# Mixture-of-experts stage of a decoder layer: expert items of 128 rows, with tails of up to 32 rows in plain fp32 on four column groups

## The chip, the cores and the metric

The kernel runs on one core of one Trainium2 chip. The metric is device time in microseconds of one launch of the whole layer. The kernel before takes 2739.65 us, the median of 3 runs (2737.45 to 2740.82). Below, PE is the matrix engine (PEld its weight loads), DVE the vector engine, ACT the scalar engine, POOL the GpSimd engine and SP the sync engine, which here issues the weight DMAs.

## The reference

One decoder layer on 1024 tokens of 1024 channels, in fp32: dilated attention beside a causal convolution, an output projection, a mixture of 32 experts of which each token takes 4, and a per-layer embedding at the end. Only the mixture of experts changes:

```python
logits = (xt @ w_router + b_router).astype(jnp.float32)
top_val, top_idx = lax.top_k(logits, TOP_K)          # 4 of 32 experts a token
gates = jax.nn.softmax(top_val, axis=-1)
...                                                   # tokens are grouped by expert
gu = rows @ w_gate_up[e] + b_gate_up[e]               # (rows, 1024) @ (1024, 2048)
gate = jnp.minimum(gu[:, :D_FF], SWIGLU_LIMIT)
up = jnp.clip(gu[:, D_FF:], -SWIGLU_LIMIT, SWIGLU_LIMIT)
hid = (up + 1.0) * (gate * jax.nn.sigmoid(gate * SWIGLU_ALPHA))
return hid @ w_down[e] + b_down[e]                    # (rows, 1024) @ (1024, 1024)
```

Each row of an expert's result goes back to its token, times its gate. 1024 tokens times 4 give 4096 rows over 32 experts, 128 a piece in the mean. With the reference's own inputs the counts of the experts 0 to 31 are 133, 123, 110, 68, 179, 71, 131, 118, 88, 121, 203, 58, 81, 65, 249, 125, 94, 133, 109, 240, 126, 118, 149, 112, 160, 135, 167, 130, 23, 235, 109, 133 (worked out from the reference on the host; they give 46 blocks of 128, as many as the trace shows row stores).

## The kernel before, in words

The stages run one after the other: input norm and projections, attention with the convolution beside it, output projection and router (until about 780 us), experts (780 to 2526 us), output (to the end). Names and lines below are those of the listing at the end of this section.

**Items.** After the router, DVE builds a table of items from the counts (lines 1817 to 1862): an item is an expert with up to 256 of its rows (`BLK`), that is one or two blocks of 128. Every engine walks the same table in a loop (`Items.run`, line 473): two outer steps of `GROUP` = 32 items each, the second skipped when item 32 is not alive, and an inner `If` for each item that isn't. `TWO` says that an item has a second block, and for it the engine runs the body with blocks `(1, 0)`, otherwise with `(0,)`. Here there are 32 items, 14 of them with two blocks.

**Pieces.** The weights of an item come in 12 pieces of 1 MB into 6 buffers `raw`: pieces 0 to 7 are half of the contraction for 256 gate and 256 up columns (`gate_piece`), pieces 8 to 11 a quarter of the contraction of the down projection (`down_piece`). SP loads a piece when DVE has read its buffer (line 978). A matmul of fp32 precision is made of three in a faster format: ACT rounds a piece to `whi` (`split_hi`, line 1447, up to 6 ahead), DVE takes the difference to `wlo` (`split_lo`, line 709, up to 4 ahead), the rows are split in the same way (`xhi`, `xlo`), and `three` (lines 550 to 552) multiplies hi by hi, lo by hi and hi by lo. A block therefore takes, for each item, 12 matmuls of 128x512 a piece, a bias row (line 544) for each of six results, 8 transposes of its rows (`turn_rows`, line 521) and 8 of its hidden values (`turn_hidden`, line 529).

**Order.** It is written out by hand as steps c = 0 to 11 on every engine. After piece c, PE gives `w_free`; on that ACT splits piece c + 6 and DVE piece c + 4. Between these splits stand, in the same order for each item, the clamps, the sigmoid (ACT), the gating (DVE) and the split of the turned hidden values. ACT and DVE are in-order, so a split that waits holds up the small operations behind it. POOL fetches the row numbers and gathers the rows of the next item (lines 1069 and 1071), and ACT stores the results of a block (`rows_out`, line 1476).

Of the kernel before, what the change touches and what calls it, by code (L numbers as in the profile page):

```python
# [18 lines left out]
P = 128  # L19
# [27 lines left out]
BLK = 2 * P  # L47
MAX_ITEMS = E + T * TOPK // (BLK + 1)
# [27 lines left out]
def layer(nc, x, p_in, positions, g_mix_pre, w_in, w_dw, b_dw, g_conv_ln, b_conv_ln, w_out, g_mix_post,  # L76
# [3 lines left out]
    with outer:  # L80
# [10 lines left out]
        def banks(b, n=1):  # L91
# [5 lines left out]
        list_dram = nc.dram_tensor("token_list", (E * T, 1), I32, kind="Internal").ap()  # L97
        y_dram = nc.dram_tensor("expert_rows", (MAX_BLOCKS * P, D), F32, kind="Internal").ap()
# [112 lines left out]
        xhi = sb("xhi", [P, 2, KD, P], F32R)  # L211
        xlo = sb("xlo", [P, 2, KD, P], F32R)
        hhi = sb("hhi", [P, 2, KD, P], F32R)
        hlo = sb("hlo", [P, 2, KD, P], F32R)
        xg = sb("xg", [P, 2, D])
        ysb = sb("ysb", [P, 2, D])
        gat = sb("gat", [P, 2, 256])
        upc = sb("upc", [P, 2, 256])
        sig = sb("sig", [P, 2, 256])
        hid = sb("hid", [P, 2, 2, 256])  # L220
        bsp = sb("bsp", [P, 3 * D], F32R)
        one_r = sb("one_r", [P, P], F32R)
        ids = sb("ids", [P, 2], I32)
# [108 lines left out]
        gu_done = sem("gu_done1")  # L332
        gu_used = [sem(f"gu_used{b}") for b in range(2)]
        gat_ready = [sem(f"gat_ready{b}") for b in range(2)]
        sig_done = [sem(f"sig_done{b}") for b in range(2)]
        gs_done = [sem(f"gs_done{b}") for b in range(2)]
        hid_ready = [sem(f"hid_ready{b}") for b in range(2)]
        ht_done = [sem(f"ht_done{b}") for b in range(2)]
        hhi_ready = [sem(f"hhi_ready{b}") for b in range(2)]
        hlo_ready = [sem(f"hlo_ready{b}") for b in range(2)]  # L340
        y_done = [sem(f"y_done{b}") for b in range(2)]
        y_used = [[sem(f"y_used{b}{d}") for d in range(2)] for b in range(2)]
        y_out = [sem(f"y_out{b}") for b in range(2)]
        ids_in = [sem(f"ids_in{b}") for b in range(2)]
        xg_in = [sem(f"xg_in{b}") for b in range(2)]
        xt4_done = [sem(f"xt4_done{b}") for b in range(2)]
        xhi_ready = [sem(f"xhi_ready{b}") for b in range(2)]
        xlo_ready = [sem(f"xlo_ready{b}") for b in range(2)]
# [30 lines left out]
        ITEM_MAX = {EXPERT: E - 1, ROW: E * T - BLK, TWO: 1, NTWO: MAX_ITEMS, LIVE: 1, BEFORE: MAX_ITEMS,  # L379
                    YROW: (MAX_BLOCKS - 2) * P}  # L380
# [12 lines left out]
        TWO_STEP = 37  # L393
        TABLE_STEP = 43
# [64 lines left out]
        class Items:  # L459
# [17 lines left out]
            def run(self, body):  # L477

                eng = self.eng
                with eng.Fori(0, 2) as o:  # L480
                    with eng.If(read(eng, o * GROUP, LIVE) > 0):
                        with eng.Fori(o * GROUP, o * GROUP + GROUP) as n:
                            live, two = self.value(LIVE), self.value(TWO)
                            k1 = eng.snap(self.twos, min_val=0, max_val=MAX_ITEMS)
                            with eng.If(live > 0):
                                with eng.If(two > 0):
                                    body(n, k1, (1, 0))
                                    eng.reg_add(self.twos, self.twos, 1)
                                with eng.Else():
                                    body(n, k1, (0,))  # L490

        def gate_bank(blocks, b, q):
            return banks(2 * b + q % 2) if len(blocks) == 2 else banks(2 + q % 2)

        def down_bank(b, d):
            return banks(2 * b + d)
# [13 lines left out]
        def experts_pe(pe):  # L510

            pe.wait_ge(bias_zero, 2)

            def turn_rows(b, k, other, before):

                pe.wait_ge(xg_in[b], 16 * k + 16)

                if before is not None:
                    pe.wait_ge(xlo_ready[other], before)
                for j in range(KD):  # L520
                    mm = pe.transpose(banks(4, 2)[:, j * P:j * P + P], xg[:, b, j * P:j * P + P], ident)  # L521
                mm.then_inc(xt4_done[b], 1)
# [1415 lines left out]
```

## Time and profile before

| | |
|---|---|
| median of 3 runs | 2739.65 us (2737.45 to 2740.82) |
| profiled execution, its own time | 2739.35 us |
| its span (first to last instruction) | 2737.7 us |
| busy PE / DVE / ACT / POOL | 2504.0 / 1736.6 / 1316.9 / 200.8 us |
| granted TensorE clock, mean of the span | 0.961 of 2.4 GHz (1.00 in the expert stage from 840 us) |
| chain that ended last, share by engine | PE 80%, DVE 7%, issue 6%, DMA 3% |
| moved by DMA | 556.34 MB, mean 203 GB/s |

How to read it: an engine's busy time is what its own instructions take, without waits; matmuls overlap, so a matmul that is listed with 390 ns may start 227 ns after the one ahead of it. The chain is followed back from the last instruction, at each step to what released it; its shares say where a shorter instruction would have shortened the whole. The share of the DMA engines is a mean over 16; where it stands at 1.00 or above, transfers wait for each other.

### The profile page before, as it was taken

The numbers are of one execution on the slowest core, as the hardware profiler recorded it, in microseconds if no ns is written. First come the engines' busy times: TensorE is split into PE (matmuls) and PEld (weight loads), VectorE is DVE, ScalarE is ACT, GpSimd is POOL, SyncE is SP. The second block draws the span as 40 slices with busy tenths as digits, with TensorE's granted clock in tenths as the row PEclk, the third lists the DMA queues.
The fourth block names the chain that finished last, engine by engine and source line by source line (L and its number), as shares of the span: only waits on it lengthen the run. The fifth ranks groups of instructions, "written<-read, shape, count | busy, mean of one in ns | idle before, by whom it ended". The sixth has DMA issues, their size and how long they took to land.

```text
span 2737.7 us, 36956 instructions
## 1 busy us (share of the span) xinstructions
PE 2504.0 (91%) x10955; PEld 1803.4 (66%) x10956; DVE 1736.6 (63%) x2495; ACT 1316.9 (48%) x1535; POOL 200.8 (7%) x188
## 2 busy tenths in 40 slices
PE   7999999768829999999999999999999999998687
PEld 3454555434428778787877878787878888776343
DVE  4664555623356986779688696778675667674454
ACT  2113344422124775567477574666554445562232
POOL 1100100002220000000000000000000000000210
PEclk9999999888859999999999999999999999999799
DMA  5009610333225996789699696879675667783541
GB/s 178 20 12 334 197 28 13 110 104 69 61 93 170 348 343 218 253 285 369 211 340 343 224 339 214 293 250 334 219 268 201 207 206 241 244 284 132 181 144 50
DMA packets 387537, 556.34 MB, mean 203 GB/s; under 512 B 18241, under 2 KB 326977, under 8 KB 387362
## 3 DMA queue, kind: packets, MB, share of 16 engines
q1 hardware_dynamic: 333922, 456.55, 50.2%
q10 hardware_dynamic: 39408, 57.67, 5.8%
q0 software_dynamic: 14160, 41.51, 4.5%
q8 instruction: 27, 0.44, 0.1%
q14 instruction: 20, 0.16, 0.0%
HBM read 482.91 MB, written 71.19 MB: 202 GB/s over the span
## 4 chain that ended last, share of the span: by engine, by line
PE 80%; DVE 7%; issue 6%; DMA 3%; ACT 2%; SPq 1%; DVEq 1%; ACTq 0%; POOLq 0%; POOL 0%
PE bank L552 16%; PE bank L550 16%; PE bank L551 16%; PE bank L1120 6%; PE bank L1264 5%; PE bank L645 4%; PE bank L1143 3%; PE bank L1110 2%; PE bank L544 2%; PE bank L1160 2%; PE bank L1189 2%; PE bank L1175 1%; PE bank L521 1%; PE bank L529 1%; DVE wlo L709 1%
## 5 line engine op out<-in xcount | busy, mean ns | idle before, releaser
L1447 ACT ACTIVATE whi<-raw 128x2048 fp32r<-128x2048 f32 x384 | 733.1, 1917 | 578.0 <-PE bank L552 531.8
L709 DVE TENSOR_TENSOR wlo<-raw,whi 128x2048 fp32r<-128x2048 f32 x384 | 875.9, 2285 | 209.2 <-PE bank L552 194.1
L550 PE MATMUL bank<-whi,xhi 128*128 128x512 f32 x1472 | 577.1, 392 | 0.0
L552 PE MATMUL bank<-wlo,xhi 128*128 128x512 f32 x1472 | 574.3, 390 | 0.0
L551 PE MATMUL bank<-whi,xlo 128*128 128x512 f32 x1472 | 573.7, 390 | 0.0
L552 PEld LDWEIGHTS bank<-wlo,xhi 128*128 128x128 f32 x1472 | 276.4, 188 | 58.2
L551 PEld LDWEIGHTS bank<-whi,xlo 128*128 128x128 f32 x1472 | 276.6, 188 | 57.0
L550 PEld LDWEIGHTS bank<-whi,xhi 128*128 128x128 f32 x1472 | 276.9, 188 | 54.2
L550 PE MATMUL bank<-whi,hhi 128*128 128x512 f32 x736 | 292.2, 397 | 0.0
L552 PE MATMUL bank<-wlo,hhi 128*128 128x512 f32 x736 | 287.4, 391 | 0.0
L551 PE MATMUL bank<-whi,hlo 128*128 128x512 f32 x736 | 286.9, 390 | 0.0
L725 DVE TENSOR_SCALAR gat<-bank 128x256 f32<-128x256 f32 x184 | 77.7, 422 | 149.2 <-PE bank L552 149.2
L552 PEld LDWEIGHTS bank<-wlo,hhi 128*128 128x128 f32 x736 | 138.1, 188 | 29.7
L551 PEld LDWEIGHTS bank<-whi,hlo 128*128 128x128 f32 x736 | 138.4, 188 | 27.1
L550 PEld LDWEIGHTS bank<-whi,hhi 128*128 128x128 f32 x736 | 138.4, 188 | 25.8
L1264 PE MATMUL bank<-uT,mixS 128*128 128x512 f32 x256 | 129.4, 670 | 16.8 <-DMA gffn<-in_g_ffn_pre_dram 16.8
L645 PE MATMUL bank<-raw,h2T 128*128 128x512 f32 x256 | 120.1, 625 | 19.4 <-DVE ple L829 16.6
L1069 POOL DMA_DIRECT2D ids<-token_list x46 | 26.1, 568 | 1345.2 <-PE bank L521 1314.2
L544 PE MATMUL bank<-bsp,one_r 128*128 128x512 f32 x276 | 116.1, 421 | 0.4 <-issue 0.4
L1645 DVE CUSTOM_DVE_ANT_0 S<-bank,mlog 128x512 f32<-128x512 f32 (+3 forms) x144 | 72.9, 553 | 64.1 <-PE bank L1160 41.0
L1264 PEld LDWEIGHTS bank<-uT,mixS 128*128 128x128 f32 x256 | 54.9, 218 | 86.1 <-issue 86.1
L1364 ACT ACTIVATE PT<-bank 128x512 f32<-128x512 f32 (+3 forms) x96 | 44.5, 514 | 136.5 <-PE bank L1175 136.5
(261 smaller groups left out, 2837.9 us busy)
## 6 DMA issues: line engine op xcount, KB each, us to landing
raw<-in_w_gate_up_dram SPq DMA_DIRECT2D x512, 512.0 KB, 4.5
raw<-in_w_down_dram SPq DMA_DIRECT2D x128, 1024.0 KB, 5.8
expert_rows<-zeros ACTq DMA_DIRECT2D x1, 32768.0 KB, 103.5
expert_rows<-ysb ACTq DMA_DIRECT2D x46, 512.0 KB, 6.2
xall<-in_x_dram SPq DMA_DIRECT2D x8, 512.0 KB, 10.5
uT<-in_w_out_dram SPq DMA_DIRECT2D x1, 4096.0 KB, 13.3
xr<-in_x_dram SPq DMA_DIRECT2D x8, 512.0 KB, 6.8
h_scratch<-h SPq DMA_DIRECT2D x8, 512.0 KB, 2.7
```

Of the source, the lines that this page charges most:

```text
L544: mm = pe.matmul(dst, one_r[:], bsp[:, q * 512:q * 512 + 512], start=True, stop=False)
L550: pe.matmul(dst, stat_hi[:, b, kt], hi, start=False, stop=False)
L551: pe.matmul(dst, stat_lo[:, b, kt], hi, start=False, stop=False)
L552: return pe.matmul(dst, stat_hi[:, b, kt], lo, start=False, stop=last)
L645: pe.matmul(banks(4 + half), h2T[:, k], wpg[:, k, half * 512:half * 512 + 512], start=(k == 0), stop=(k == KD - 1))
L709: dve.tensor_tensor(wlo[:, c % LO], raw[:, c % RAW], whi[:, c % HI].bitcast(F32), ALU.subtract).then_inc(lo_ready, 1)
L725: dve.tensor_scalar(gat[:, b], src[:, 0:256], LIMIT, None, ALU.min).then_inc(gat_ready[b], 1)
L1120: mm = pe.matmul(banks(bank_no), w[:, k], uT[:, k, half * 512:half * 512 + 512], start=(k == 0), stop=(k == KD - 1))
L1143: mm = pe.matmul(banks(b + c)[:, 0:n], uT[:, k, t * P:t * P + P], wv[:, k, c * 512:c * 512 + n], start=(k == 0), stop=(k == KD - 1))
L1264: mm = pe.matmul(banks(2 * s + half), mixS[s][:, k], wout[:, k, half * 512:half * 512 + 512], start=(k == 0), stop=(k == KD - 1))
L1447: act.activation(whi[:, c % HI], raw[:, c % RAW], ACT.Copy).then_inc(hi_ready, 1)
L1645: dve.tensor_tensor_reduce(out=S[b][:, c * 512:c * 512 + w], in0=banks(2 * c + h)[:, 0:w], in1=mlog[:, T - n + c * 512:T - n + c * 512 + w ...
```

## The change: what it does

An item is now one block of up to 128 rows, and may have a tail of up to 32 rows. An expert with n rows gets ceil(n / 128) items, but where its last one would hold 32 rows or fewer they go as a tail with the item ahead of it (the thresholds are 160, 288, ... instead of 256, 512, ...). `TWO` and `NTWO` now say whether there is a tail and how many came before. The second set of row buffers is gone, and with it the body for two blocks.

The tail takes the weights straight from `raw` in plain fp32, without the split. It has 32 rows, so its transposed rows are a weight load of 128x32, and four such products stand beside each other on the four groups of 32 columns of the array: in pieces 0 to 7 group j takes contraction tile j of the piece, all four give partial sums of the same 512 columns, and a further matmul with a constant `sel` adds the four; in pieces 8 to 11 group j takes output columns 256j to 256j + 255. Gate and down biases come by DMA into `bias_t` and `bias_d`. The tail's piece c + 4 (`AHEAD`) follows main piece c on PE; tail pieces 0 to 3 therefore stand in pieces 8 to 11 of the item ahead, under an `If`. SP frees a buffer when the tail has read it, too. The list of token numbers, the results' buffer and a few table steps grow accordingly.

```diff
-BLK = 2 * P
-MAX_ITEMS = E + T * TOPK // (BLK + 1)
+TAIL = 32
+GROUPS = P // TAIL
+MAX_ITEMS = E + T * TOPK // (P + TAIL + 1)
...
+        XT, SUM, HT, ACC = 4, 5, 6, 7
+        AHEAD = 4
...
+            def tail_piece(n, k1, c):
+                pe.wait_ge(hi_ready, PIECES * n + c + 1)
+                if c == 0:
+                    pe.wait_ge(xt_ready, k1 + 1)
+                    pe.wait_ge(ytail_ready, k1)
+                if c in (2, 4, 6, 8):
+                    pe.wait_ge(sums_ready, 4 * k1 + c // 2)
+                if c >= 8:
+                    pe.wait_ge(ht_ready, 4 * k1 + c - 7)
+                if c < 8:
+                    half = c % 2
+                    for j in range(GROUPS):
+                        mm = pe.matmul(banks(ACC)[j * TAIL:j * TAIL + TAIL, :], xt[:, half * 4 + j], raw[:, c % RAW, j],
+                                       start=(half == 0), stop=(half == 1))
+                else:
+                    r = c - 8
+                    for kk in range(2):
+                        for j in range(GROUPS):
+                            mm = pe.matmul(banks(ACC)[j * TAIL:j * TAIL + TAIL, 0:256], htail[:, 2 * r + kk],
+                                           raw[:, c % RAW, 2 * kk + j // 2, j % 2 * 256:j % 2 * 256 + 256],
+                                           start=(r == 0 and kk == 0), stop=(r == 3 and kk == 1))
+                mm.then_inc(tail_free, 1)
+            def tail_sum(n, k1, j):
+                pe.wait_ge(sums_ready, 4 * k1 + j + 1)
+                pe.wait_ge(xlo_ready, n + 1)
+                pe.wait_ge(hid_t_ready, 4 * k1 + j)
+                pe.matmul(banks(SUM)[0:TAIL, :], sel[:], sums[:], start=True, stop=True).then_inc(u_done, 1)
+            def turn_tail_hidden(k1, j):
+                hold(pe, hid_t_ready, 4 * k1 + j + 1)
+                hold(pe, ht_ready, 4 * k1 + j)
+                for h in range(2):
+                    mm = pe.transpose(banks(XT)[:, h * TAIL:h * TAIL + TAIL], hid_t[0:TAIL, h * P:h * P + P],
+                                      ident[0:TAIL, 0:TAIL])
+                mm.then_inc(htt_done, 1)
...
+            def body(n, k1, tail):                                  # PE
+                nk1 = k1 + tail
+                for c in range(PIECES):
+                    pe.wait_ge(lo_ready, PIECES * n + c + 1)
+                    mm = gate_piece(n, c) if c < 8 else down_piece(n, c)
+                    mm.then_inc(w_free, 1)
+                    if c in (3, 5, 7):
+                        turn_hidden(n, (c - 3) // 2)
+                    if tail and c in (0, 2, 4, 6):
+                        turn_tail_hidden(k1, c // 2)
+                    if tail and c in (0, 2, 4):
+                        tail_sum(n, k1, c // 2 + 1)
+                    if tail and c + AHEAD < PIECES:
+                        tail_piece(n, k1, c + AHEAD)
...
+                    if c + AHEAD >= PIECES:
+                        with pe.If(nxt2 > 0):
+                            tail_ahead(n + 1, nk1, c + AHEAD - PIECES)
...
+            def tail_sums(k1, j):                                   # DVE
+                if j == 0:
+                    dve.wait_ge(bias_t_in, 16 * k1 + 16)
+                dve.wait_ge(u_done, 4 * k1 + j)
+                dve.wait_ge(tail_free, PIECES * k1 + 2 * j + 2)
+                dve.tensor_tensor(sums[:].rearrange("p (h n) -> p h n", h=2),
+                                  banks(ACC).rearrange("p (h n) -> p h n", h=2),
+                                  bias_t[:].rearrange("p (h q n) -> p h q n", h=2, q=4)[:, :, j, :],
+                                  ALU.add).then_inc(sums_ready, 1)
...
+                    if tail and c in (1, 3, 5):
+                        tail_gated(k1, (c + 1) // 2)
+                    if tail and c in (1, 3):
+                        tail_sums(k1, (c + 3) // 2)
+                    if tail and c in (0, 2, 4):
+                        tail_clamp(k1, c // 2 + 1)
...
+                                read_by_tail = sp.snap(tails * PIECES + two * (c + 1), ...)   # SP
+                                hold(sp, lo_ready, PIECES * n + c + 1)
+                                sp.wait_ge(tail_free, read_by_tail)
...
+            pool.memset(bias_t[:], 0.0).then_inc(tail_zero, 1)      # POOL, once
```

ACT has a copy for each turned tail tile (`tail_columns`, `tail_hidden`), a sigmoid for each quarter (`tail_sigmoid`) and four DMAs for a tail's result. `tail_clamp`, `tail_gated` and `tail_rows` on DVE are the counterparts of `clamp`, `gated` and the copy of the result.

On PE, in the body for an item with a second part, this stands behind the first piece (lines 550 to 552 are `three`, 544 the bias row). Before, the same piece is run for block 0:

```order
L552 MATMUL bank<-wlo,xhi 128x512
L560 REGISTER_ALU [waits y_used00]
L544 MATMUL bank<-bsp,one_r 128x512 [waits bias_in0,xlo_ready0]
L550 MATMUL bank<-whi,xhi 128x512
L551 MATMUL bank<-whi,xlo 128x512
L552 MATMUL bank<-wlo,xhi 128x512
```

After, in its place (583 is the last line of `three`, 652 turns the tail's hidden values, 646 adds its partial sums, 630 is its piece 4, x3 after the one that waits):

```order
L583 MATMUL bank<-wlo,xhi 128x512
L420 ISA
L652 MATMUL bank<-cst,hid_t 128x32 [waits hid_t_ready,ht_ready]
L652 MATMUL bank<-cst,hid_t 128x32
L643 REGISTER_ALU
L646 MATMUL bank<-sums,sel 32x512 [waits hid_t_ready,xlo_ready,sums_ready]
L619 REGISTER_ALU
L630 MATMUL bank<-raw,xt 32x512 [waits sums_ready,hi_ready]
L630 MATMUL bank<-raw,xt 32x512 x3
```

Thirteen matmuls of 128x512 have gone; seven small instructions, two of which wait for DVE, have come.

On DVE, the same body, step c = 1. Before (709 is the split of the weights, 725 and 726 the clamps, 730 and 737 the gating):

```order
L725 TENSOR_SCALAR gat<-bank 128x256 [waits hid_ready0]
L726 TENSOR_SCALAR upc<-bank 128x256
L708 REGISTER_ALU [waits w_free]
L709 TENSOR_TENSOR wlo<-raw,whi 128x2048 [waits hi_ready]
L730 TENSOR_TENSOR sig<-gat,sig 128x256 [waits sig_done1]
L737 SCALAR_TENSOR_TENSOR hid<-upc,sig 128x256 [waits ht_done1,gs_done1]
```

After (803 and 804 clamp, 790 splits the weights, 841 and 845 gate the tail, 827 takes its partial sums):

```order
L803 TENSOR_SCALAR gat<-bank 128x256 [waits hid_ready]
L804 TENSOR_SCALAR upc<-bank 128x256
L789 REGISTER_ALU [waits w_free]
L790 TENSOR_TENSOR wlo<-raw,whi 128x2048 [waits hi_ready]
L841 TENSOR_TENSOR sig_t<-gat_t,sig_t 32x256 [waits sig_t_done]
L845 SCALAR_TENSOR_TENSOR hid_t<-upc_t,sig_t 32x256 [waits htt_done,gs_t_done]
L826 ISA [waits u_done]
L827 TENSOR_TENSOR sums<-bank,bias_t 128x512 [waits tail_free]
```

The tail's gating and sums now stand behind a split of 2.3 us on the same engine.

## Rows read from the trace of the kernel before

**Rows 1.** Groups by line, 800 to 2526 us: busy, mean ns | idle before, releaser.
```profile
L709 DVE TENSOR_TENSOR wlo<-raw,whi 128x2048 fp32r<-128x2048 f32 x384 | 875.9, 2285 | 209.2 <-PE bank L552 194.1 <-issue 14.3
```
**Rows 2.** ACT timeline: row stores of items 4, 5, 6 to 9, 24, 25; end.
```profile
1079.06 0.34 ACTq L1476 DMA_DIRECT2D expert_rows<-ysb  x1
...
1119.40 0.35 ACTq L1476 DMA_DIRECT2D expert_rows<-ysb  x1
...
1189.74 0.34 ACTq L1476 DMA_DIRECT2D expert_rows<-ysb  x1
...
1226.65 0.42 ACTq L1476 DMA_DIRECT2D expert_rows<-ysb  x1
...
1263.62 0.41 ACTq L1476 DMA_DIRECT2D expert_rows<-ysb  x1
...
1305.86 0.35 ACTq L1476 DMA_DIRECT2D expert_rows<-ysb  x1
...
2083.75 0.34 ACTq L1476 DMA_DIRECT2D expert_rows<-ysb  x1
...
2156.49 0.34 ACTq L1476 DMA_DIRECT2D expert_rows<-ysb  x1
...
2524.46 1.28 ACT L658 ACT_TABLE_LOAD   x1 [3.98 <-issue]
```
**Rows 3.** Windows: us, PE PEld DVE ACT POOL busy, clock, DMA share, GB/s.
```profile
1226.65:1263.62 36.97, 36.65 (x168) 29.48 (x167) 34.91 (x34) 29.89 (x25) 2.52 (x3) 1.00 1.07 370
...
2132.00:2205.00 73.00, 72.30 (x335) 59.55 (x334) 44.72 (x55) 34.69 (x38) 2.53 (x3) 1.00 0.61 201
...
960.00:1020.00 60.00, 56.30 (x257) 45.35 (x256) 49.01 (x46) 42.48 (x36) 4.21 (x5) 1.00 1.02 353
```
**Rows 4.** PE timeline in a block: two matmuls in a row.
```profile
1227.05 0.39 PE L552 MATMUL bank<-wlo,xhi 128*128 128x512 f32 x1
1227.28 0.39 PE L550 MATMUL bank<-whi,xhi 128*128 128x512 f32 x1
```
**Rows 5.** The DMA view, 1226 to 1263 us: rate in 40 slices, packets.
```profile
GB/s 357 331 324 321 380 422 425 412 421 416 412 412 412 412 403 407 421 380 374 350 349 347 350 350 344 349 351 344 350 351 358 334 327 344 352 344 350 352 350 373
DMA packets 9710, 13.65 MB, mean 369 GB/s; under 512 B 416, under 2 KB 8367, under 8 KB 9708
```
**Rows 6.** Timelines of item 9: ACT waits for a load, DVE for ACT.
```profile
1271.05 1.92 ACT L1447 ACTIVATE whi<-raw 128x2048 fp32r<-128x2048 f32 x1 [1.68 <-DMA raw<-in_w_gate_up_dram]
...
1274.73 0.42 DVE L730 TENSOR_TENSOR sig<-gat,sig 128x256 f32<-128x256 f32 x1 [3.14 <-ACT sig L1455]
```
**Rows 7.** PE timeline in attention: plain fp32 matmuls (out columns * rows).
```profile
243.55 1.98 PE L1120 MATMUL bank<-uT,wk 128*128 128x512 f32 x4
245.37 0.27 PE L1175 MATMUL bank<-cst,S 128*128 128x128 f32 x1
...
247.64 1.53 PE L1189 MATMUL bank<-PT,raw 128*64 128x128 f32 x24
249.10 1.12 PE L1120 MATMUL bank<-uT,wk 128*128 128x512 f32 x2
```
**Rows 8.** Groups by form on PE, whole span: plain fp32 matmuls alone.
```profile
L1120 PE MATMUL bank<-uT,wq 128*128 128x512 f32 x192 | 91.7, 605 | 0.1
...
L1143 PE MATMUL bank<-xall,uT 128*128 128x256 f32 x128 | 28.9, 379 | 0.0
```
**Rows 9.** Groups by form on DVE, expert stage: small operations.
```profile
L737 DVE SCALAR_TENSOR_TENSOR hid<-upc,sig 128x256 f32<-128x256 f32 x184 | 78.3, 425 | 6.3
...
L714 DVE TENSOR_TENSOR xlo<-bank,xhi 128x1024 fp32r<-128x1024 f32 x46 | 56.2, 1221 | 19.4 <-ACT xhi L1451 19.4
```
**Rows 10.** PE timeline at the stage's start: the second turn waits for its gather.
```profile
817.40 1.97 PE L521 MATMUL bank<-cst,xg 128*128 128x128 f32 x8 [6.47 <-DMA xg<-u_scratch,ids]
819.74 0.79 PE L544 MATMUL bank<-bsp,one_r 128*128 128x512 f32 x1 [0.37 <-issue]
```
**Rows 11.** PE's waits, 822 to 2520 us.
```profile
PE bank L521 <- DVE xlo L714: 19.8, 13, 1.8
```

More of the change, by code:

```diff
@@ L331, in layer @@
         w_free = sem("w_free")
[L332 to L348, printed above, removed]
+        gu_used = sem("gu_used")
@@ L747, in experts_dve, with body @@
             for c in range(LO):
                 split_lo(0, c)
+            columns(0)
             with dve.If(items.value(TWO) > 0):
-                columns(1, 0)
-            columns(0, 0)
-            def body(n, k1, blocks):
-                nk1 = k1 + (len(blocks) - 1)
+                for c in range(AHEAD):
+                    tail_ahead(0, c)
+            def body(n, k1, tail):
+                nk1 = k1 + tail
                 for c in range(PIECES):
+                    if tail and c == 8:
+                        tail_rows(k1)
@@ L1478, in _, with tail_rows_out @@
+            def tail_rows_out(k1, row):
+                act.wait_ge(ytail_ready, k1 + 1)
+                for j in range(GROUPS):
+                    act.dma_start(y_dram[bass.ds(row + P, TAIL), j * 256:j * 256 + 256],
+                                  ysb_t[j * TAIL:j * TAIL + TAIL]).then_inc(ytail_out, 16)
             items = Items(act, "act", (LIVE, TWO))
             for c in range(HI):
+                if c == 4:
+                    with act.If(items.value(TWO) > 0):
+                        tail_columns(0)
+                    columns(0)
@@ L1517, in body @@
                         nxt, nxt2 = items.value(LIVE), items.value(TWO)
-                    if c == 10:
+                    if tail and c == 9:
+                        tail_rows_out(k1, row)
+                    if c == 11:
                         with act.If(nxt2 > 0):
-                            columns(0, n + 1)
+                            tail_sigmoid(nk1, 0)
             items.run(body)
-            stored = [read(act, P - 1, what) * 16 for what in (BEFORE, NTWO)]
-            for b in range(2):
-                act.wait_ge(y_out[b], stored[b])
+            stored = read(act, P - 1, BEFORE) * 16, read(act, P - 1, NTWO) * 64
+            act.wait_ge(y_out, stored[0])
+            act.wait_ge(ytail_out, stored[1])
             act_fin(act)
```

471 lines of the change are left out of this document (273 added, 198 removed).

## The prediction

> **What bounds the kernel now.** I read the page first: PE 80% of the chain that ended last, so PE it is; then the marks of the items, then windows over single items. The change touches the expert stage alone. Its PE work runs from the first bias row at 819.74 us to the last block's end, about 2519.9 us, just ahead of the end of ACT's last copy (2524.46 - 3.98) [rows 2, 10]: 1700 us. In it stand 32 items, 18 of one block and 14 of two, 46 blocks. What a block costs is read from the stores. Items 24 and 25, both of two blocks, end 2156.49 - 2083.75 = 72.74 us apart, 36.4 a block; item 8, of one block, takes 1263.62 - 1226.65 = 36.97 us [rows 2]. 46 x 36.4 = 1674, and 26 us are left; most are one wait: where a two-block item follows, PE waits for DVE's xlo (19.8 us, 13 times) [rows 11].
>
> So PE is full in both kinds of item (36.65 busy of 36.97, 72.30 of 73.00) [rows 3], with a matmul each 0.227 us [rows 4]. But with one block there is no slack elsewhere either: DVE is busy 34.9 us of 36.97, and the DMA share stands at 1.07, against 0.61 with two blocks [rows 3]. The loads of one item need 13.65 MB in 37 us, at 350 GB/s in the gate pieces and about 412 in the down pieces [rows 5]. A third item of one block in a row shows what comes of it: ACT waits 1.68 us for a load, its sigmoid is late, DVE waits 3.14 us for that [rows 6].
>
> **The change part by part.**
>
> *Items.* By the counts in the reference section 14 experts have over 128 rows. Eight have 160 or fewer (0, 6, 17, 22, 24, 25, 27, 31) and get one item with a tail; six (4, 10, 14, 19, 26, 29) get two items and load their weights twice. So 38 items instead of 32, 38 blocks instead of 46, 8 tails. 30 items have no tail. Per PE the eight blocks save 8 x 36.4 = 291 us, and per DMA six loads more are 82 MB. DMA was at 0.61 with two blocks; now most items are of the kind that needs all of it.
>
> *An item without a tail.* The first after slack takes 36.9 (1226.65 - 1189.74), the second 36.97 [rows 2]. The third (item 9) took 42.24 to its store, but that holds the ending before a two-block item, with its xlo wait; item 5, the same ending with no one-block item ahead, took 1119.40 - 1079.06 = 40.34 [rows 2], so 1.9 us is what the late sigmoid cost. That makes 38.8. From the fourth on, DMA sets the pace: 13.65 MB at the 369 GB/s of this window is 37.0 us, and at the 353 GB/s of a mixed window [rows 3, 5] 38.7; I take 37.4, near the window that is all of one item. The order of experts gives runs without a tail of 6, 12, 5, 1, 2 and 4 items: 225 + 449 + 187.5 + 37 + 74 + 150 = 1122 us. The xlo wait goes with the second set of rows: now the rows are turned at c = 7 and needed at the next item's c = 0. New branches on PE I cost at nothing: the branches behind c = 7 and c = 9 of today leave it busy for 36.65 of 36.97 us [rows 3], so its sequencer reads ahead.
>
> *A tail on PE.* Three rows bound a plain fp32 matmul. Four of 128x512 start at 243.55 and the next thing at 245.37: 0.43 us each with the change-over, so twice 512 columns at 2.4 GHz. 24 of 64 columns of weights and 128 moving, in two column groups, take 249.10 - 247.64 = 1.46 us, 0.061 each, where one in the whole array takes 0.107 by the same two cycles a column: two groups do run side by side [rows 7]. Four groups are not in the trace. Bounds for the four matmuls of a tail piece: 0.43 us, if side by side, and 4 x 0.43 = 1.7, one after the other. I take 0.43, as the two groups behave, and 0.2 for changing in and out of the narrow form (1.46 - 24 x 0.054 = 0.16 in the row named). 12 pieces x 0.63 = 7.6 us (a down piece has eight of 256 columns, two rounds of 0.215, the same). Four sums at 0.43 + 0.1: 2.1. 16 turns of 32 rows at 0.06 and five change-overs: 2.0. Together 11.7 us.
>
> The Trainium skill (FP8 and Floating Point Precision, on true fp32) says that it makes 4 passes through the array; the row above shows the time of two. By the page's figure the 12 pieces and 4 sums would take 16 x 0.43 = 6.9 us more a tail, and the whole 55 us more, about 2647. The Trainium skill (TensorEngine Tiling, key properties) also says that changing the tiling mode drains the engine; that is the change-over above, and the trace agrees that it is small.
>
> *The tail's waits.* Each quarter goes PE pieces, DVE sums, PE sum, DVE clamp, ACT sigmoid, DVE gating, PE turn, ACT copy, and DVE and ACT reach their parts only behind a split of 2.29 and 1.92 us [rows 1, 6]. Counted from the end T of the item ahead: ACT stores and splits, then the tail's sigmoid ends at T + 3.9, DVE's gating (two of 0.42 [rows 9]) at T + 4.75, its sums (0.65, half of the 1.22 for 1024 columns) at T + 5.4. PE is there after tail piece 3 and main piece 0 at T + 3.6: it waits 1.6 us. At c = 2 the same count gives 1.5 (the sigmoid's table load, 1.28 like the one in [rows 2], stands in the way), at c = 4 0.5 and at c = 6 0.3. 3.9 us together, bounds 0 and twice that. DVE has 34.9 + 8.6 us of work in some 52, so it is not the bound of a tail item.
>
> A tail item is therefore 36.9 + 11.7 + 3.9 = 52.5 us, the tail 15.6. Eight: 420 us.
>
> *Start and end.* DVE's table has five steps more and POOL sets bias_t: 3 us ahead of the first fetch. At the start PE waited for the second gather (turned from 817.40) [rows 10]. Now the tail's rows are that second gather, and behind them stand four tail pieces with a trip to DVE, before main piece 0: 7 us more, less the 3 us of tail work that the 420 already hold. Outer step two has 6 live items and 26 dead ones, each three or four instructions of the sequencer, which no row shows; the last store's landing hides the first 3.98 us of that [rows 2]. I take 3 us, bounds 0 and 10. POOL's fetches for a tail, its broadcasts and the four stores move 0.64 MB beside an item of 52 us: nothing. SP's wait on the tail costs nothing, since the tail reads a buffer 4 pieces before the main rows, at the time of DVE's split.
>
> *Sum.* 1122 + 420 - 3 + 7 + 3 + 3 = 1552 us against 1700: 148 us less. The profiled execution's own 2739.35 (span 2737.7 and 1.65 around it) is 0.3 below the median of the runs, so 2739.5 - 148 = 2592 us.
>
> **The rivals.**
>
> *The loads bound every item.* For it: share 1.07, ACT's wait for loads in the second and third item of a run. Against: 369 GB/s is just what an item needs. Runs of 6 and 12 items have no double block to refill the buffers. At 353 GB/s, 38.7 us an item: 30 x 1.3 = 39 more, 2631. Long waits in the tail's round (doubled, 31 us) give the same, 2623.
>
> *The tail is cheaper.* ACT and DVE slip ahead and PE never waits for them, and no item without a tail takes over 37: 31 + 15 less, 2546.
>
> *Column groups take turns.* Weight loads of four groups or the shared bank keep them apart. 32 x 0.43 + 32 x 0.215 = 20.6 instead of 5.2 us a tail: 8 x 15.4 = 123 more, 2715. Against: the two groups of attention.
>
> *Slower than before.* Place: the tail pieces on PE. Mechanism: the groups neither overlap nor pipeline, since all write one bank, so each matmul takes its full 605 or 379 ns [rows 8]: 32 x 0.605 + 32 x 0.379 = 31.5 instead of 5.2, 8 x 26.3 = 210 more, 2802. It decides from 18.5 us more a tail on. For it: four groups accumulate into the same bank. Against: attention's 24 do so in pairs at 0.061 each.
>
> *The change doesn't do what it says:* other counts on the chip, so more items or fewer tails. The 46 blocks and the places of the two-block items agree with the counts, so I give it nothing of its own.
>
> **How the numbers follow.** Forecast 2592 (its own range 2565 to 2620): 52%. Loads or waits longer, 2620 to 2665: 21%. Cheaper tail, 2540 to 2565: 13%. Groups in turn: 7%. The page's four passes, 2647: 2%, against the row. Slower: 5%. The range 2545 to 2660 leaves out the last two large cases and some of the edges. Faster by over 0.2% 94%, within 0.2% (what a measurement of this kernel can tell from no change) 1%, slower 5%.
>
> **What would show it.** 38 row stores in the stage, runs of them 37 to 39 us apart, tail items 50 to 55; DMA share at 1 nearly throughout and clock at 1.00. Tail matmuls of 32x512: four starting within 0.5 us. PE's waits: none for xlo, some 30 us for the tail's gating and sums. I am wrong if one-block items settle well over 38 us, if four tail matmuls take over 1 us, or if PE's waits in a tail item pass 8 us.

## The result, and the profile after

Before: 2740.24 us median of 4 runs (2737.45 to 2741.53). After: 2652.10 us median of 4 (2651.18 to 2655.26). The ratio is 0.9682 with a 95% interval of 0.9665 to 0.9698: 88 us less, where 148 were forecast. The time lies inside the range of 2545 to 2660, near its upper end, and 60 us above the forecast of 2592. The profiled execution took 2655.26 us with a span of 2653.3; its working below is made against its own time, 63.9 us above the forecast's 2591.35 for such an execution.

In the page after, PE is busy for 90% of the span, and the chain of waits still runs mostly over it, with issue (an engine that waits for nothing the profile shows) second:

```profile
PE 2386.5 (90%) x10843; PEld 1603.3 (60%) x10844; DVE 1884.2 (71%) x2573; ACT 1452.9 (55%) x1604; POOL 242.4 (9%) x229
...
PE 69%; issue 10%; DVE 9%; DMA 5%; ACT 4%; DVEq 1%; SPq 1%; ACTq 1%; POOL 0%; POOLq 0%
```

What answers to the row stores of [rows 2] is ACT's timeline again. First the stores around one tail item: the tail's four (x4), then the item's own, then those of two items without a tail.

```profile
1161.13 2.16 ACTq L1636 DMA_DIRECT2D expert_rows<-ysb_t  x4
1167.01 0.36 ACTq L1630 DMA_DIRECT2D expert_rows<-ysb  x1
1203.95 0.37 ACTq L1630 DMA_DIRECT2D expert_rows<-ysb  x1
1241.84 0.35 ACTq L1630 DMA_DIRECT2D expert_rows<-ysb  x1
...
2027.26 0.36 ACTq L1630 DMA_DIRECT2D expert_rows<-ysb  x1
...
2080.09 0.36 ACTq L1630 DMA_DIRECT2D expert_rows<-ysb  x1
```

There are 38 such stores. The first item after a tail takes 36.94 us, the next 37.89; a tail item after another takes 2080.09 - 2027.26 = 52.83; an item ahead of a tail, which holds four of its pieces, takes about 43.0 (an item ended at 2117.03 and the next, ahead of a tail, at 2160.08). The windows, with the columns of [rows 3] (us; PE, PEld, DVE, ACT, POOL busy; clock, DMA share, GB/s), of one item, of a tail item with four pieces of the next tail, and of ten items without one:

```profile
1203.95:1241.84 37.89, 36.88 (x168) 29.42 (x167) 34.87 (x34) 30.01 (x25) 2.59 (x2) 1.00 1.05 364
1970.00:2027.00 57.00, 54.77 (x317) 34.11 (x315) 42.94 (x55) 31.83 (x34) 4.46 (x7) 1.00 0.72 241
1205.00:1575.00 370.00, 361.42 (x1632) 288.77 (x1631) 341.75 (x328) 295.25 (x247) 23.00 (x20) 1.00 1.05 363
```

PE is busy for 361.42 of 370 us without tails, so 0.87 us of an item is idle, where [rows 3] had 0.32 in one. The new groups on PE, by form, 780 to 2450 us:

```profile
L630 PE MATMUL bank<-raw,xt 128*32 128x512 f32 x512 | 86.0, 615 | 0.0
...
L636 PE MATMUL bank<-raw,htail 128*32 128x256 f32 x512 | 39.0, 385 | 0.0
L646 PE MATMUL bank<-sums,sel 128*32 128x512 f32 x64 | 33.5, 605 | 2.1 <-DVE sums L827 0.9
L652 PE MATMUL bank<-cst,hid_t 32*128 32x32 f32 x64 | 9.1, 222 | 15.9 <-DVE hid_t L845 15.9
```

Here the counts are the thing to see. Eight tails have eight gate pieces of four matmuls, which is 256 of L630; the trace has 512. They have 32 sums (L646); it has 64. The order of the program shows "L630" once and then x3 in a piece (in the part on the change), the timeline shows x8:

```profile
1973.23 0.28 PE L652 MATMUL bank<-cst,hid_t 32*128 32x32 f32 x2 [0.58 <-DVE hid_t L845]
1973.59 0.62 PE L646 MATMUL bank<-sums,sel 128*32 128x512 f32 x1
1973.80 0.63 PE L630 MATMUL bank<-raw,xt 128*32 128x512 f32 x3
1974.05 0.59 PE L646 MATMUL bank<-sums,sel 128*32 128x512 f32 x1
1974.25 1.25 PE L630 MATMUL bank<-raw,xt 128*32 128x512 f32 x5
1975.43 0.50 PE L581 MATMUL bank<-whi,xhi 128*128 128x512 f32 x1
...
1978.38 1.06 PE L630 MATMUL bank<-raw,xt 128*32 128x512 f32 x8
1979.37 0.50 PE L575 MATMUL bank<-bsp,one_r 128*128 128x512 f32 x1
```

A plain fp32 matmul is recorded twice; the transposes, L570 with 304 rows for 38 x 8 and L652 with 64 for 8 x 8, are recorded once. The piece alone takes 1979.37 - 1978.38 = 0.99 us and the sum with a piece 1975.43 - 1973.59 = 1.84. The two rows of L646 start 0.46 apart; the first three of L630 stand between them. The sum goes to column group 0, so these are presumably rows for the other groups, but a row doesn't name its group.

The start and the end of the stage answer to [rows 10] and to the last row of [rows 2]. PE, then ACT:

```profile
816.81 3.29 PE L630 MATMUL bank<-raw,xt 128*32 128x512 f32 x16
821.03 0.62 PE L646 MATMUL bank<-sums,sel 128*32 128x512 f32 x1 [0.92 <-DVE sums L827]
...
823.72 0.50 PE L575 MATMUL bank<-bsp,one_r 128*128 128x512 f32 x1
...
2419.30 0.39 PE L583 MATMUL bank<-wlo,hhi 128*128 128x512 f32 x1
2437.42 0.47 PE L703 MATMUL bank<-cst 128*128 128x128 f32 x1 [17.73 <-issue]
```

```profile
2420.48 0.36 ACTq L1630 DMA_DIRECT2D expert_rows<-ysb  x1
2440.24 1.28 ACT L736 ACT_TABLE_LOAD   x1 [19.92 <-issue]
```

The first main bias row comes 4 us later than the 819.74 of before, the last matmul ends at about 2419.5. So the stage takes 1596 us instead of 1700. Behind it ACT was idle for 3.98 us before and is now for 19.92. That makes -104 + 4 + 16 = -84, the difference of the spans (2653.3 - 2737.7).

### The profile page after: what moved, and what is told of

Its sections match the earlier page's. It is cut to its first block, busy times and chain, and to the rows that moved or that the text cites. A ratio compares the mean times of both kernels' runs of the same rounds, so it can differ in the third digit from the quotient of the medians.

```text
span 2653.3 us, 40578 instructions
## 1 busy us (share of the span) xinstructions
PE 2386.5 (90%) x10843; PEld 1603.3 (60%) x10844; DVE 1884.2 (71%) x2573; ACT 1452.9 (55%) x1604; POOL 242.4 (9%) x229
## 4 chain that ended last, share of the span: by engine, by line
PE 69%; issue 10%; DVE 9%; DMA 5%; ACT 4%; DVEq 1%; SPq 1%; ACTq 1%; POOL 0%; POOLq 0%
PE bank L581 11%; PE bank L583 11%; PE bank L582 11%; PE bank L1267 6%; PE bank L1411 5%; PE bank L723 4%; PE bank L1290 3%; DMA raw<-in_w_down_dram 3%; DVE wlo L790 2%; PE bank L1257 2%; PE bank L630 2%; PE bank L1307 2%; PE bank L575 1%; PE bank L1336 1%; PE bank L553 1%
## 5 line engine op out<-in xcount | busy, mean ns | idle before, releaser
L1594 ACT ACTIVATE whi<-raw 128x2048 fp32r<-128x2048 f32 x456 | 871.4, 1916 | 382.6 <-PE bank L583 296.1
L790 DVE TENSOR_TENSOR wlo<-raw,whi 128x2048 fp32r<-128x2048 f32 x456 | 1036.3, 2284 | 50.2 <-PE bank L583 40.2
L581 PE MATMUL bank<-whi,xhi 128*128 128x512 f32 x1216 | 479.6, 394 | 0.0
L583 PE MATMUL bank<-wlo,xhi 128*128 128x512 f32 x1216 | 475.8, 391 | 0.0
L582 PE MATMUL bank<-whi,xlo 128*128 128x512 f32 x1216 | 475.7, 391 | 0.0
L581 PEld LDWEIGHTS bank<-whi,xhi 128*128 128x128 f32 x1216 | 229.5, 189 | 63.9 <-issue 19.7
L582 PEld LDWEIGHTS bank<-whi,xlo 128*128 128x128 f32 x1216 | 229.2, 188 | 48.2
L581 PE MATMUL bank<-whi,hhi 128*128 128x512 f32 x608 | 243.2, 400 | 0.0
L582 PE MATMUL bank<-whi,hlo 128*128 128x512 f32 x608 | 237.8, 391 | 0.0
L583 PE MATMUL bank<-wlo,hhi 128*128 128x512 f32 x608 | 237.4, 390 | 0.0
L581 PEld LDWEIGHTS bank<-whi,hhi 128*128 128x128 f32 x608 | 114.3, 188 | 38.7 <-issue 17.6
L808 DVE TENSOR_TENSOR sig<-gat,sig 128x256 f32<-128x256 f32 x152 | 63.5, 418 | 64.5 <-ACT sig L1607 64.5
L803 DVE TENSOR_SCALAR gat<-bank 128x256 f32<-128x256 f32 x152 | 63.9, 421 | 59.4 <-PE bank L583 59.4
```

What stands on the lines that cost most here:

```text
L581: pe.matmul(dst, stat_hi[:, kt], hi, start=False, stop=False)
L582: pe.matmul(dst, stat_lo[:, kt], hi, start=False, stop=False)
L583: return pe.matmul(dst, stat_hi[:, kt], lo, start=False, stop=last)
L790: dve.tensor_tensor(wlo[:, c % LO], raw[:, c % RAW], whi[:, c % HI].bitcast(F32), ALU.subtract).then_inc(lo_ready, 1)
L803: dve.tensor_scalar(gat[:], src[:, 0:256], LIMIT, None, ALU.min).then_inc(gat_ready, 1)
L808: dve.tensor_tensor(sig[:], gat[:], sig[:], ALU.mult).then_inc(gs_done, 1)
```

## The experiments

**Groups of 8.** The items' loop runs in two groups of 32, of which the second holds 6 live items and 26 dead ones.

```diff
-GROUP = 32
+GROUP = 8
...
-                with eng.Fori(0, 2) as o:
+                with eng.Fori(0, 8) as o:
```

The loops of SP and POOL, which are written out by themselves, change in the same way.

> The loop over items runs in 8 groups of 8 instead of 2 of 32, on every engine; nothing else changes. Theory (dead iterations): in the changed kernel PE, DVE and ACT stand idle 17.7, 15.7 and 19.9 us between the last item and the next stage, which is 26 dead iterations at some 0.69 us on PE's sequencer. 38 items now leave 2 dead ones in the fifth group, so the idle time falls to about 4 us and the kernel gains 14 to 16 us: 2637. Rival (the end waits for the last tail's store or for loading code): the idle time stays near 18 us and the time within 3 us of 2652; five more outer steps could also cost some 0.5 us each at item boundaries, 2655.

Measured: 2645.13 us (2644.31 to 2649.05), ratio 0.9657 (0.9641 to 0.9673), 7 us less than after. PE's idle time at the end is down from 17.73 to 2.80, and ACT's table load now waits for the store to land:

```profile
2424.53 0.32 PE L703 MATMUL bank<-cst 128*128 128x128 f32 x1 [2.80 <-issue]
```

```profile
2422.52 0.36 ACTq L1630 DMA_DIRECT2D expert_rows<-ysb  x1
2430.24 1.28 ACT L736 ACT_TABLE_LOAD   x1 [7.88 <-DMA expert_rows<-ysb]
```

From the last store to the table load is 7.7 us now and 19.8 after: 12 less. The items themselves took 3.7 us more between the first store and the last (1548.49 against 1544.83). So the 24 dead iterations that went had cost about (17.73 - 2.80) / 24 = 0.62 us each on PE, and 12 us of it was on the path. It gained 7 us where 14 to 16 were expected. The 3.7 us are about what the first items of the groups lost: the items 8, 16 and 24 (counted from 0) took 37.78, 38.58 and 40.18 us, and 36.94, 37.34 and 37.58 after; ACT waits 1.53 and 2.47 us for a gate load in the last two. Item 32, a tail item, took 52.84, and 52.81 after.

**Two of four column groups.** The tail's matmuls of groups 2 and 3 are left out, with the part of the result that they make; the loop of the down pieces is cut in the same way.

```diff
-                    for j in range(GROUPS):
+                    for j in range(GROUPS // 2):
```

> The tail's pieces issue only the matmuls of column groups 0 and 1; those of groups 2 and 3 are left out, so half of the tail's sums is missing. The changed kernel's tail piece takes 1.00 us for 8 instructions of 128x512, two for each plain fp32 matmul. Theory A (each plain matmul is two instructions of 0.43 us, and all four groups run side by side: 2 x 0.43 + 0.14): with two groups a piece still takes 1.00 us and the whole time stays at 2652 (2649 to 2655). Rival B (a plain matmul takes 0.43 us in all, and only two groups run at once): a piece falls to about 0.57 us, 12 x 0.43 x 8 = 41 us less, 2611.

Measured: 2652.68 us, a tail item 52.8, a piece 0.98 (x4 now, for two matmuls):

```profile
1977.46 1.05 PE L630 MATMUL bank<-raw,xt 128*32 128x512 f32 x4
1978.44 0.50 PE L575 MATMUL bank<-bsp,one_r 128*128 128x512 f32 x1
```

Half of the matmuls are gone and the time of a piece is not: four groups cost what two cost.

**All on one column group.** The same matmuls, one behind the other into group 0; the result is a sum of what belongs apart. The first line of the edit is shown; the down pieces change likewise, and one accumulation runs over all four.

```diff
-                        mm = pe.matmul(banks(ACC)[j * TAIL:j * TAIL + TAIL, :], xt[:, half * 4 + j], raw[:, c % RAW, j],
+                        mm = pe.matmul(banks(ACC)[0:TAIL, :], xt[:, half * 4 + j], raw[:, c % RAW, j],
```

> All four matmuls of a tail piece go to column group 0 and add up there, so the tail's output is not the reference's. Theory A: nothing can run side by side, a piece takes 8 x 0.43 + 0.14 = 3.6 us instead of 1.0, 12 x 2.6 x 8 = 250 us more, about 2900. Rival B (0.43 us for a plain matmul): 4 x 0.43 + 0.14 = 1.9, 83 us more, 2735. If the time stays near 2652, the array pays nothing for a shared group and the four groups bring nothing.

Measured: 2874.23 us, a tail item 73.42 (1220.17 - 1146.75).

```profile
1132.03 3.62 PE L630 MATMUL bank<-raw,xt 128*32 128x512 f32 x8
1135.58 0.50 PE L581 MATMUL bank<-whi,hhi 128*128 128x512 f32 x1
```

A piece takes 3.55 us: four matmuls of 0.86 and 0.1 for the change of form. By this (3.55 - 1.00) / 3 = 0.85 us is the price of one 128x32x512 matmul in plain fp32, if the four in four groups cost what one does: 0.85 and 0.14 for the change are the 1.00 measured. The whole lies 26 us below theory A's 2900. PE is now busy for all of the 73.42 us of a tail item, so its waits there went, and the item ahead of a tail grew by 8 us (43.0 to 51.1), not by four times 2.55. The column groups bring 222 us; without them the change would be a loss.

**No tails.** The thresholds go back to multiples of 128: 46 items of one block. The other thresholds (2 x 128 and so on, and the test for a tail) move in the same way, and the table has room for more items.

```diff
-            step(dve.tensor_scalar(npass[:], cnt[:], float(P + TAIL), 1.0, ALU.is_gt, ALU.add))
+            step(dve.tensor_scalar(npass[:], cnt[:], float(P), 1.0, ALU.is_gt, ALU.add))
```

> The thresholds of the item table are moved by 32 rows, so that no item has a tail: an expert of n rows gets ceil(n / 128) items, 46 in all, each with its own load of the weights. This is one part of the change, one-block items, alone. Theory (an item without a tail takes 37.6 us, set by the loads once the buffers are drained): 46 x 37.6 = 1730 us in the stage where the kernel before had 1700, plus 12 us of dead iterations (18) at the end, 2775 to 2790, slower than both. Each of the eight tails is then worth 37.6 - 21.3 = 16 us. Rival (long runs without tails drain the buffers further and items settle at 38.7 us, 353 GB/s): 2825 to 2835. Rival (PE bound at 36.9): 2750.

Measured: 2787.78 us, 46 stores 36.9 to 38.4 apart after the first two. A tail in place of an item saves (2788 - 2652) / 8 = 17 us, and splitting the two-block items into items of one block alone loses 48 us to before: a second block cost about 36.4 on PE, an item costs 37.6. About 9 us of it stand behind the last store (225.7 us to the end of the span, 217.1 before), where this table has 18 dead iterations.

**Half columns.** Each tail matmul does half of its columns (the down pieces' likewise, 128 of 256), and the tail's result lacks the others.

```diff
-                        mm = pe.matmul(banks(ACC)[j * TAIL:j * TAIL + TAIL, :], xt[:, half * 4 + j], raw[:, c % RAW, j],
+                        mm = pe.matmul(banks(ACC)[j * TAIL:j * TAIL + TAIL, 0:256], xt[:, half * 4 + j], raw[:, c % RAW, j, 0:256],
```

> The tail's matmuls do half of their columns (256 of 512 against the gate and up pieces, 128 of 256 against the down ones), the rest of the tail's columns is left out; counts, waits and change-overs stay. It asks whether the 1.00 us of a tail piece is a price per column. Theory A, two instructions of two cycles a column each, four cycles a column: a piece goes from 1.00 to 0.57 us, 12 x 0.43 = 5.2 us a tail, 41 us in all, about 2612 (up to 2630 if PE then waits longer for ACT and DVE in the tail item). Rival B, a fixed price per instruction or for the change between the forms: a piece stays near 1.00 and the whole near 2652.

Measured: 2635.47 us. The piece does what theory A says, 1.00 to 0.57 us:

```profile
1944.48 0.64 PE L630 MATMUL bank<-raw,xt 128*32 128x256 f32 x8
1945.05 0.50 PE L581 MATMUL bank<-whi,hhi 128*128 128x512 f32 x1
```

0.43 us for 256 columns are four cycles a column at 2.4 GHz, and the 0.14 left over are the change of form. But the whole fell by 17 us, not by 41, nor by the 22 that I had allowed for: PE's waits in the tail, by the same view as after, took much of it back.

```profile
L646 PE MATMUL bank<-sums,sel 128*32 128x512 f32 x64 | 33.3, 601 | 6.6 <-DVE sums L827 4.8
...
L652 PE MATMUL bank<-cst,hid_t 32*128 32x32 f32 x64 | 8.9, 219 | 26.5 <-DVE hid_t L845 25.7
```

The waits grew by 4.5 and 10.6 us, 15 of the 24 missing. A tail takes 51.25 - 36.94 = 14.3 us in its item and 42.4 - 37.6 = 4.8 in the item ahead, 19.1, of which PE works 17.2 - 12 x 0.43 = 12.0 and is idle for 7.1. So over a third of this cheap tail is PE waiting for the round over ACT and DVE.

**The tail's small operations first.** Shown is the first edit on ACT; DVE's gating and sums move likewise from behind `split_lo` to ahead of it, and the first quarter's to ahead of the split at c = 11.

```diff
+                    if tail and c in (1, 3, 5):
+                        tail_sigmoid(k1, (c + 1) // 2)
...
-                    if tail and c in (1, 3, 5):
-                        tail_sigmoid(k1, (c + 1) // 2)
```

> ACT's sigmoid of a tail quarter stands ahead of the next split instead of behind it, and so do DVE's gating and sums of the tail. It asks whether the 3.2 us that PE waits in a tail item (the largest ahead of the turn of 32 rows, 15.9 us in all) is the time that the short tail operations stand behind a split. Theory A: yes, PE's wait for hid_t goes from 15.9 to under 5 us and the splits have slack in an item of 52 us: 10 to 20 us less, about 2638. Rival B: the splits that are now behind the tail's operations come late for the main rows, the wait moves from L652 to the main matmuls (for wlo or whi), the whole within 5 us of 2653 or above.

Measured: 2631.81 us (2629.47 to 2635.34), ratio 0.9610 (0.9593 to 0.9628), 20 us less than after, at the upper end of theory A. The turn no longer waits (L652: 15.9 us of idle time ahead of it after, 0.0 now); a tail item takes 50.32 us instead of 52.8.

```profile
1957.17 0.39 PE L583 MATMUL bank<-wlo,xhi 128*128 128x512 f32 x1
1957.49 0.31 PE L652 MATMUL bank<-cst,hid_t 32*128 32x32 f32 x2
1957.73 0.62 PE L646 MATMUL bank<-sums,sel 128*32 128x512 f32 x1
```

**Both together, and groups of 20.** The early order with groups of 8, then with groups of 20.

> The order of the run before with the items' loop in groups of 8 instead of 32 (2 dead iterations instead of 26). If the two edits are independent, as both theories of them say, the gains add: 7 us for the groups and what the order alone brings, so about 2631 if that is 14. Rival: the groups of 8 cost PE its read-ahead at each outer step just where the tail's order has become tight, and less than 7 is added.

Measured: 2623.90 us (2622.78 to 2628.69), ratio 0.9581 (0.9561 to 0.9600). It adds 7.9 to the early order's 20.3, where groups of 8 alone brought 7.0: within the scatter of the runs the two gains add.

> The order of the early run, with the items' loop in groups of 20 (one boundary between groups among the 38 items instead of four, and again 2 dead iterations). It asks where the 3 to 4 us went by which the items of groups of 8 took longer in all. Theory A, each boundary between groups costs about a us (the test of a live item and a new loop on every engine's sequencer): 2 to 3 us less than groups of 8, about 2621. Rival B, that difference is scatter between executions: within 1 us of 2624.

Measured: 2620.79 us (2617.97 to 2624.86), ratio 0.9567 (0.9554 to 0.9580). That is 3.1 less than groups of 8, as theory A says, but the intervals overlap. The items tell more: with groups of 8 the items 8, 16 and 24 took 38.00, 39.74 and 38.76 us, against 36.93, 37.81 and 38.16 in the early order alone, and the only first item that groups of 20 add is a tail item, 50.32 us in both. So in these two executions of groups of 8 a boundary costs 0.6 to 2.6 us at an item without a tail and nothing at one with a tail. This is the fastest of all kernels run, 31 us below after.

**Half of the down loads.** What sets an item without a tail at 37.6 us?

```diff
-                sp.dma_start(dst.rearrange("p (k d) n -> p k (d n)", k=2), rows).then_inc(raw_in[slot], 16)
+                sp.dma_start(dst.rearrange("p (k d) n -> p k (d n)", k=2)[:, 0:1], rows[:, 0:1]).then_inc(raw_in[slot], 16)
```

> Half of every down piece's load is left out (the first half of each slot is loaded, the rest of the buffer keeps what was there), so an item loads 10.5 MB less 0 for the gate pieces and 2.1 MB less for the down ones. It asks what sets the 37.6 us between stores of items without a tail. Theory A, the loads: ACT's waits of 0.8 us for a load in such an item go, the items settle at PE's 36.9, the whole comes out 15 to 25 us lower, about 2632. Rival B, the engines' hand-overs (ACT and DVE behind each other, not the loads) set it: the items stay at 37.6, the whole within 5 us of 2653.

Measured: 2648.59 us. The same window as above, 1205 to 1575 us:

```profile
1205.00:1575.00 370.00, 361.40 (x1630) 288.56 (x1629) 341.39 (x328) 294.62 (x247) 23.72 (x20) 1.00 0.90 306
```

The DMA share fell from 1.05 to 0.90 and PE's busy time did not move by 0.1 us. Ten items took 377.1 us (376.7 after). This is rival B's number, but not its cause: the edit left whole what these items wait for. In the window ACT waits 6.6 us for gate loads and 0.2 for down loads after, 6.8 and 0 now, and in the first 6 us of an item, when the last gate load is under way, the DMA share is still 1.07 (1203.48 to 1209.48 us; 0.56 from 1215.48 to 1221.48). The chain in one item of 37.90 us of the kernel after, on SP, ACT and PE, then the same wait with the down loads halved, in an item of 37.94:

```profile
1276.80 0.37 SPq L476 DMA_DIRECT2D raw<-in_w_gate_up_dram  x1
...
1285.32 1.92 ACT L1594 ACTIVATE whi<-raw 128x2048 fp32r<-128x2048 f32 x1 [0.89 <-DMA raw<-in_w_gate_up_dram]
...
1289.94 0.44 PE L570 MATMUL bank<-cst,hid 128*128 128x128 f32 x2 [0.67 <-DVE hid L812]
```

```profile
1436.19 1.92 ACT L1594 ACTIVATE whi<-raw 128x2048 fp32r<-128x2048 f32 x1 [0.90 <-DMA raw<-in_w_gate_up_dram]
```

Item by item it comes out the same in the kernel after: without this wait an item takes 36.90 or 37.00 us (37.14 once), with 0.30 us of it 37.34, with 0.76 us 37.77, with 0.89 us 37.90, with 1.32 us 38.33. With the down loads halved it is 36.93 with none and 38.88 with 1.85, and in the run without tails 36.90 with none and 38.29 with 1.27. Only the first item behind a tail can wait and still take 36.94. So one gate load, the item's last (piece 7), does set the time of an item without a tail; the down loads don't.

Where the down loads do count is ahead of a tail. ACT waits 2.2 to 2.5 us for one in most of these items after, and at most 0.5 in four of them with half the load; four of the items are 1.1 to 1.4 us shorter then. Ahead of the tail of expert 24 it is more:

```profile
1936.48 1.93 ACT L1594 ACTIVATE whi<-raw 128x2048 fp32r<-128x2048 f32 x1 [3.67 <-DMA raw<-in_w_down_dram]
```

PE stands still for 2.69 us there and the mean clock granted over that item is 0.96; it takes 46.01 us, and 41.97 at a clock of 1.00 with the loads halved. The item ahead of the last tail went the other way (45.94 for 42.93, with a wait of 2.32 for a gate load). From the first store to the last 5.5 us were gained, in a single run.

## Why the prediction was right in sign and short in size

**Right: the structure.** 38 items, 8 tails, no wait for xlo, the clock at 1.00 in the items shown, DMA at 1.05. The column groups run side by side and the two rivals against that (in turn, 2715; unpipelined, 2802) are refuted by leaving groups out and by stacking them.

**The term that failed: "0.43 us each", for a plain fp32 matmul of 512 columns.** From [rows 7] the prediction read four matmuls between 243.55 and 245.37. They were two. L1120 runs over 6 pairs, 2 halves and 8 tiles for wq, 96 matmuls, and [rows 8] counts 192: each has two rows in the trace, so it costs 0.86 us. (The 24 rows of L1189 in [rows 7] are twelve matmuls in the same way, 0.12 us each where one alone would take four cycles for each of 128 columns, 0.21: that two groups run side by side stands.) The prediction then set this misreading against the Trainium skill (FP8 and Floating Point Precision, TensorE Precision Notes), which gives four passes through the array. The Trainium skill was right, and the trace agrees once its rows are counted: 0.85 us for 512 columns, and 0.43 us less for 256 columns less. The case that the prediction had priced by that rule at 2647, and given 2%, lies 5 us below the median; that closeness is partly luck, since the price is worth 46 us by the sum below and not the 55 of that case, and other misses fill the gap.

By its own steps a tail measures on PE: 12 pieces at 1.00 (0.63 forecast) are 12.0; 4 sums at 1.84 - 0.99 = 0.85 (0.53) are 3.4; turns and changes 0.61 + 4 x 0.3 = 1.8 (2.0). Together 17.2 instead of 11.7. The change of form, 0.14 us a piece where 0.2 was taken, was near enough.

**The tail's waits: right in size only beside the wrong price.** The item ahead of a tail has 43.0 - 37.6 = 5.4 us of it and the tail item 52.83 - 36.94 = 15.9, so 21.3 in all, and 21.3 - 17.2 = 4.1 is idle, where 3.9 were forecast. The cause was in part as the prediction put it: the tail's sigmoid and gating stand behind a split. PE's rows have (15.9 + 2.1) / 8 = 2.3 us a tail ahead of the turns and the sums, and the early order took 2.5 us away. Of the rest, some 1.4 us a tail are what the items ahead of four tails lost to a wait for a down load, which stands nowhere in the prediction's round; this sum is rough. But with a piece at 0.57 us, less than the 0.63 of the prediction, PE is idle for 7.1, near the upper bound of twice 3.9, and the kernel takes 2635, not 2592. At the price that I took, my waits were too short by about 3 us a tail: the matmuls' real length covered them. So the price explains all of the 46 us as the kernel stands, and yet its correction alone would have brought back only 17; the forecast needed cheap pieces and the early order both.

**Items without a tail: right, for the reason given, in another form.** Measured mean 37.6, forecast 37.4. The prediction let the loads set it from the fourth item on, at a mean rate. What the trace shows is the chain of [rows 6] in small, in most items from the second of a run on: ACT waits 0.3 to 1.3 us for the last gate load, its sigmoid is late, DVE waits for that and PE for DVE.

```profile
DVE sig L808 <- ACT sig L1607: 64.5, 36, 2.7
...
PE bank L570 <- DVE hid L812: 11.7, 18, 1.1
```

(DVE's and PE's waits, 822 to 2425 us: in total, times, longest.) The item takes 36.9 us and the wait for the load, to within 0.25 us. SP issues that load at the same place in the items compared, 1.9 to 2.0 us ahead of the store, whether ACT then waits or not, so what differs is the time that the load takes to land, 8.0 us from issue to ACT's start in the item above, at most 7.1 in the one of 36.90. Why it takes that long, with half of the down loads gone too, is open, and no run changed the gate loads. The rival that the loads cost every item 38.7 us did not come.

**The end: 3 us forecast with bounds of 0 and 10, 16 measured.** A dead iteration was taken as a few instructions that the store's landing hides. It costs 0.62 us on PE, and 26 of them outlast the landing.

**The start: 10 forecast, 4 measured**, since the tail's rows are there earlier than the second gather was, and its pieces stand in a single stretch, 816.81 to 823.72, with one wait of 0.92.

**Not foreseen: item 1.** Its store comes 43.49 us after the first, 6.5 more than the 36.94 of other items behind a tail. PE is idle for 3.82 us ahead of it, and then runs at the lower level, 1.2 GHz, for some 5 us, with 0.43 us from matmul to matmul. The last line is the window from 879 to 884 us, with the columns of [rows 3]:

```profile
874.47 0.39 PE L583 MATMUL bank<-wlo,hhi 128*128 128x512 f32 x1
878.68 0.79 PE L575 MATMUL bank<-bsp,one_r 128*128 128x512 f32 x1 [3.82 <-DVE wlo L790]
...
879.70 0.63 PE L582 MATMUL bank<-whi,xlo 128*128 128x512 f32 x1
880.13 0.63 PE L583 MATMUL bank<-wlo,xhi 128*128 128x512 f32 x1
```

```profile
879.00:884.00 5.00, 5.00 (x13) 3.85 (x13) 0.00 (x0) 0.00 (x0) 0.00 (x0) 0.50 1.02 395
```

The wait, and thirteen matmuls in 5.7 us instead of 3.0 (the next starts at 884.39), make up the 6.5. An obvious guess is the first entry into the body without a tail. The run without tails contradicts that, since all of its items use this body, and its item 1 took 46.46 us with a longer idle time, put down to issue:

```profile
863.24 0.79 PE L575 MATMUL bank<-bsp,one_r 128*128 128x512 f32 x1 [6.89 <-issue]
```

In both it is the step from the first turn of the items' loop to the second; what holds PE there stays open.

The 63.9 us, summed: tails 8 x 5.7 = 46, less 2.4 for the first one, whose ahead part stands before the stage (5.4 taken off where 3 were); items 30 x 0.2 = 6; item 1, 5.9 above 37.6; the item ahead of the tail of expert 24, 3 above the others ahead of a tail; end 13; start -6. That is 65.5, or 1.6 too much.

Of the prediction's own signs, two came out otherwise. Four tail matmuls do not start within 0.5 us, a piece takes 1.00, right at the bound that was to show it wrong. PE's waits for the tail's gating and sums are 18 us by its rows, not 30. One-block items stayed under 38 in the mean, and PE's waits in a tail item under 8.

## What to carry to other kernels

Before a duration per instruction becomes a price, count the rows of its group against what the loops of the code issue: a plain fp32 matmul stands there twice, and two starts 0.43 us apart were one matmul of 0.86. Where the Trainium skill states a rule and a row seems to contradict it by a clean factor of two, suspect the count first. When an experiment takes loads away and nothing moves, look in the trace whether the wait for a load moved: here half of the down loads went, and the wait was for a gate load. Narrow work (32 rows) in plain fp32 pays if it is spread over the four column groups, and once it is short the engines around it set a good part of its time: put its small operations ahead of the long ones they would queue behind. A loop with a fixed number of turns isn't free in its empty ones; size its groups so that few are left.

## What the hardware showed unexpectedly

- Four matmuls on four column groups of 32 took 1.00 us, two on two groups 0.98, four in one group 3.55. One matmul is 0.85 by the last, with 0.14 for the change of form.
- Rows of L630 start between the two rows of a sum in group 0 (L646 in the timeline above), and the sum adds 0.85 us, one matmul's price. A plain fp32 matmul has two rows, a transpose of fp32 one.
- An empty loop iteration, whose test skips the body, took about 0.62 us on PE's sequencer.
- Leaving out a sixth of the loads (363 to 306 GB/s), all from the down pieces, gave the items without a tail nothing, though one late load sets their time: 36.9 us and ACT's wait for the last gate load, 0 to 1.3 us. The mean DMA share (1.05, then 0.90) told neither.
